# Attention heads in pairs with V stationary, and the output projection moved to a stage of its own

## The reference, cut to what matters

```python
oa = band_attend(qa, ka, va, ...)            # own chunk and 8 before: at most 640 keys a tile, bias table
score = sum_h wi[h] * relu(qi[h] . ki)       # indexer; keep the 256 best keys of each query
ob = softmax(qb . kb / 8 + t5_bias, on the kept keys) @ vb     # all keys up to the tile's end
y  = x + gate1 * rmsnorm(concat(oa, ob) @ w_out)
h  = rmsnorm(y) * (1 + scale2) + shift2
y  = y + gate2 * rmsnorm(swiglu(h, w_gate, w_up, w_down))
```

## Time and profile before

| | us |
|---|---|
| median of three runs (1856.07 to 1862.26) | 1858.51 |
| the profiled execution, its own time | 1858.22 |
| its span, first to last instruction | 1856.4 |
| PE busy, 9145 matmul rows | 1712.2 |
| DVE / ACT / POOL busy | 819.1 / 658.0 / 173.6 |
| mean granted PE clock, share of full speed | 0.961 |

### The profile page before, as it was taken

How to read it: one execution, slowest core, us unless ns; L and a number is a source line. 1 busy time by engine, 2 the same in 40 slices (tenths; PEclk the granted TensorE clock), 3 DMA queues, 4 the chain that set the end, 5 groups by cost and what they waited for, 6 DMA issues and landing times. The chain is left out here.

```text
span 1856.4 us, 23651 instructions
## 1 busy us (share of the span) xinstructions
PE 1712.2 (92%) x9145; PEld 1372.6 (74%) x9145; DVE 819.1 (44%) x1601; ACT 658.0 (35%) x1215; POOL 173.6 (9%) x299
## 2 busy tenths in 40 slices
PE   4998899999799988899999299999999999999997
PEld 0543899964578755566654299999999999787876
DVE  2111566668899865554432411111111111455454
ACT  2100445545899823333322511111111111343433
POOL 3001000033111011221100100000000000102020
PEclk9999899999799979999999699999999999999999
DMA  9445511140000030000000411111111111643442
GB/s 345 190 169 189 146 46 35 35 138 1 1 2 1 2 139 23 23 24 30 20 20 26 142 57 45 45 45 45 45 45 45 45 45 44 244 148 122 153 144 95
DMA packets 96850, 146.70 MB, mean 79 GB/s; under 512 B 12896, under 2 KB 71472, under 8 KB 94688
## 3 DMA queue, kind: packets, MB, share of 16 engines
q1 hardware_dynamic: 93408, 135.18, 21.9%
q0 software_dynamic: 3360, 10.43, 1.6%
HBM read 128.61 MB, written 18.95 MB: 79 GB/s over the span
## 5 line engine op out<-in xcount | busy, mean ns | idle before, releaser
L1408 PE MATMUL ps<-h_hi,w_hi 128*128 128x352 f32 x1056 | 341.6, 324 | 7.8 <-DVE w_lo L1448 7.8
L1408 PE MATMUL ps<-h_lo,w_hi 128*128 128x352 f32 x1056 | 339.3, 321 | 0.0
L1408 PE MATMUL ps<-h_hi,w_lo 128*128 128x352 f32 x1056 | 339.0, 321 | 0.0
L954 PE MATMUL ps<-arena 128*128 128x512 f32 (+5 forms) x464 | 183.3, 512 | 33.3 <-POOL arena L735 17.0
L1408 PEld LDWEIGHTS ps<-h_hi,w_hi 128*128 128x128 f32 x1056 | 198.9, 188 | 7.9 <-DVE w_lo L1448 7.9
L1408 PEld LDWEIGHTS ps<-h_lo,w_hi 128*128 128x128 f32 x1056 | 199.1, 189 | 0.0
L1408 PEld LDWEIGHTS ps<-h_hi,w_lo 128*128 128x128 f32 x1056 | 198.6, 188 | 0.0
L941 PE MATMUL ps<-arena 128*128 128x64 f32 (+2 forms) x1280 | 165.1, 266 | 8.5 <-DVE arena L1012 3.1
L941 PEld LDWEIGHTS ps<-arena 128*128 128x128 f32 (+2 forms) x1280 | 154.0, 185 | 13.1 <-ACT arena L1012 3.6
L1448 DVE TENSOR_TENSOR w_lo<-raw_weights,w_hi 128x1024 fp32r<-128x1024 f32 x44 | 53.6, 1221 | 233.7 <-ACT w_hi L1422 233.7
L954 PEld LDWEIGHTS ps<-arena 128*128 128x128 f32 (+1 forms) x464 | 79.1, 196 | 97.1 <-issue 66.1
(11 more groups left out here) (193 smaller groups left out, 2488.9 us busy)
## 6 DMA issues: line engine op xcount, KB each, us to landing
raw_weights<-in_w_down SPq DMA_DIRECT2D x66, 512.0 KB, 3.3
arena<-in_w_ada SPq DMA_DIRECT2D x24, 1024.0 KB, 9.8
raw_weights<-in_w_gate SPq DMA_DIRECT2D x22, 512.0 KB, 3.7
raw_weights<-in_w_up SPq DMA_DIRECT2D x22, 512.0 KB, 3.8
arena<-in_w_in SPq DMA_DIRECT2D x16, 512.0 KB, 3.7
arena<-in_x_prompt SPq DMA_DIRECT2D x4, 1024.0 KB, 18.6
arena<-in_w_out SPq DMA_DIRECT2D x2, 2048.0 KB, 10.3
arena<-in_x_prompt SPq DMA_DIRECT2D x8, 512.0 KB, 3.5
```

Source lines behind the costliest of these rows:

```text
L954: mm = nc.tensor.matmul(ps_cols(B, s_col(s) + lo, hi - lo, r), q, key_source(t, h, lo, hi), start=True, stop=True)
L1408: mm = nc.tensor.matmul(B(3 * i + c, CH), cut[i][a][:, P * k:P * k + P], h[:, NTOK * k + CH * c:NTOK * k + CH * (c + 1)], start=(k == 0 an ...
```

## The change

- **Pairs.** A step handles two heads (2c and 2c+1) of a tile: 36 pairs in place of 72 units. The queries are no longer copied into padded buffers; the product for each head uses only its own 64 partitions, head 2c on partitions 0 to 63 and head 2c+1 on 64 to 127, issued one after the other into different PSUM banks. Each head has one score area (banks 0-1, 2-3): pair s waits for both masks of pair s-1.
- **V stationary.** V (keys by 64 features) is loaded as weights and the transposed exponentials move, 128 columns (queries). The two heads' results go to partitions 0 to 63 and 64 to 127 of bank 7. They come out as [feature, token], so L1167, L979 and L1019 go; ACT copies bank 7 over the queries (`leave`).
- **Row sums.** PE transposes the 8 sums of a tile (item "R"), DVE takes the reciprocal, SP stores it to DRAM and loads it back spread over partitions, and POOL multiplies the tile in place.
- **Copies of transposed weights.** In the band part ACT copies those of the even head and DVE those of the odd one; in the sparse part ACT copies all. There are six SBUF slots in place of four.
- **Sample tile of the sparse part.** Keys 1024 to 1055 have their own ring item ("X") and their own small bias, minimum and merge.
- **`project_out`.** A new stage takes the place of the projection in the sparse part and of `ffn_input`: it loads w_out in 8 slabs of 512 KB through two buffers, cuts each (ACT high, DVE low), and per tile makes 48 fp32r products, the norms, y and the modulated, cut input of `gate_up`. One tile's head features are cut at a time.

The core of the diff:

```diff
+LAG, PV_LAG, RING_BANKS, SLOTS = 2, 2, 3, 6
+PAIRS = [(t, c) for t in range(NT) for c in range(HEADS // 2)]
...
-    pts = [KI, KI + 512, KIC, KIC + 512]
-    pbuf = [QI + 640 * i for i in range(4)] if band else [QI + NTOK * i for i in range(4)]
+    pts = [KI, KI + 512, KIC, KIC + 512] + ([QI + 3200, QI + 3712] if band else [HT, HT + 512])
+    pbuf = [QI + 640 * i for i in range(5)] if band else [QI + NTOK * i for i in range(4)] + [KA, KA + NTOK]
...
-        dve_reads = it[0] == "W" or (it[0] == "T" and it[2] > 0)
-        reader.append("v" if dve_reads else "a")
+    reader = ["a" if it[0] == "T" and (it[1] % 2 == 0 or not band) else "v" for it in items]
...
             for t in range(NT):
+                ring_read(sp, item_of[("R", t, 0, 0)])
+                sp.dma_start(d_r[t][:, 0:r], T(RT, r, HEADS)).then_inc(rinv_out, 16)
+                sp.wait_ge(rinv_out, 16 * t + 16)
+                for i in range(2):
+                    sp.dma_start(T3(BC, 4, P, HD, HD * i)[:, :, 0:r], src[:, 0:r].partition_broadcast(HD)).then_inc(rinv_in, 16)
...
-                    mm = nc.tensor.matmul(B(7, HD, r, c0=HD * h), T(pts[t_seq[q] % 4] + P * i, r, k),
-                                          value_source(t, h, b), start=(b == 0), stop=(b == blocks - 1))
+                    for i in range(2):
+                        mm = nc.tensor.matmul(B(7, r, HD, HD * i, c0=P * c), value_source(t, 2 * c + i, b),
+                                              T(pts[t_seq[qe + i] % SLOTS] + P * x, r, k), start=(b == 0), stop=(b == blocks - 1))
...
-                    pe.wait_ge(pad_ready, s + 3)
-                    q = T(pad_slot(pad, s), r)
-                    for lo, hi in pieces(0, width(t), 512):
-                        mm = nc.tensor.matmul(ps_cols(B, s_col(s) + lo, hi - lo, r), q, key_source(t, h, lo, hi),
+                    if s:
+                        pe.wait_ge(masked, 2 * s)
+                    for lo, hi in pieces(0, min(width(t), 1024), 512):
+                        for i in range(2):
+                            mm = nc.tensor.matmul(B(2 * i + lo // 512, hi - lo, r), T(q_at + NTOK * c + P * t, r, HD, HD * i),
+                                                  key_source(t, c, i, lo, hi), start=True, stop=True)
...
+def project_out(ctx, nc, ins, outs, sem, T, T3, B, view, ident, d_ada, d_y, h_hi, h_lo, raw, **_):
...
+            def load_w(c):
+                if c >= 2:
+                    sp.wait_ge(wo_lo, c - 1)
+                sp.dma_start(raw[c % 2], ins["w_out"][0][P * c:P * c + P, :]).then_inc(wo_in[c % 2], 16)
...
+        @block.tensor
...
+            for t in range(NT):
+                r = rows_of(t)
+                if t >= 2:
+                    pe.wait_ge(m_scaled, t - 1)
+                for c in range(KT):
+                    if t == 0:
+                        pe.wait_ge(wo_lo, c + 1)
+                    if c % 4 == 0:
+                        pe.wait_ge(o_lo, 2 * t + c // 4 + 1)
+                    for half in range(2):
+                        for n, (a, b) in enumerate(TERMS):
+                            mm = nc.tensor.matmul(B(2 * (t % 2) + half, 512, r), o_cut[a][:, P * c:P * c + r],
...
+                    if c % 4 == 3:
+                        mm.then_inc(half_mm, 1)
+                if t:
+                    turn(t - 1)
+            turn(SAMPLE)
+
+        @block.scalar
...
+            for t in range(NT):
+                r = rows_of(t)
+                if t + 1 < NT:
+                    first_cut(t + 1, 0)
+                    first_cut(t + 1, 1)
+                if t:
+                    act.wait_ge(turned, t)
...
+                act.wait_ge(half_mm, 2 * t + 2)
+                nc.scalar.activation(R(MB, D, r), mixed(t), ACT.Square, accum_out=T(R_SSM + t, 1, r)).then_inc(ssm_done, 1)
+                if t:
+                    h_first(t - 1)
+                act.wait_ge(y_done, t + 1)
+                nc.scalar.activation(R(MB, D, r), xb(t, r), ACT.Square, accum_out=T(R_SSY + t, 1, r)).then_inc(ssy_done, 1)
+                act.wait_ge(ry_done, t + 1)
+                act.wait_ge(ssy_done, t + 1)
+                nc.scalar.activation(R(MB, D, r), xb(t, r), ACT.Copy, scale=T(R_RY + t, 1, r)).then_inc(yn_done, 1)
...
-def ffn_input(ctx, nc, ins, outs, sem, T, T3, B, view, ident, d_y, hidden, h_hi, h_lo, raw, a_sample, **_):
```

More of the change, by code:

```diff
@@ L111, in pieces @@
     return out
[L114 to L133, removed]
 def build(nc, ins, outs):
@@ L891, in block_rows, with scores, normalised @@
         return min(P, width(t) - P * b)
[L893 to L907, removed]
+    def scores(u, n):
+        t = PAIRS[u // 2][0]
+        return B(2 * (u % 2), n, rows_of(t))
+    def normalised(eng, t):
+        eng.wait_ge(normed, t + 1)
     with nc.Block() as block:
@@ L991, in _ @@
+                if s >= NP + LAG and pending:
                     pv(pending.pop(0))
         def read_item(eng, name, q):
-            it = items[q]
-            bank = 4 + q % RING
+            kind, u, b0, nb = items[q]
+            bank = 4 + q % RING_BANKS
             eng.wait_ge(ring_mm, q + 1)
@@ L998, in read_item @@
             done = ring_act if name == "a" else ring_dve
-            if it[0] == "T":
-                _, u, b0, nb = it
-                t = units[u][0]
+            if kind == "T":
+                t = PAIRS[u // 2][0]
                 r = rows_of(t)
                 i = t_seq[q]
-                if i >= 4:
-                    eng.wait_ge(pv_mm, i - 3)
-                full = [b for b in range(nb) if block_rows(t, b0 + b) == P]
-                part = [b for b in range(nb) if block_rows(t, b0 + b) < P]
-                dst, src = T(pts[i % 4], 512), B(bank, 512)
-                assert not (full and part), "a ring item is full blocks or one partial block"
-                if full:
-                    copy(view(dst, [[P, len(full)], [1, r]]), view(src, [[P, len(full)], [1, r]])).then_inc(done, 1)
+                if i >= SLOTS:
+                    eng.wait_ge(pv_mm, i // 2 - SLOTS // 2 + 1)
+                dst, src = T(pts[i % SLOTS], 512), B(bank, 512)
+                if block_rows(t, b0) == P:
+                    copy(view(dst, [[P, nb], [1, r]]), view(src, [[P, nb], [1, r]])).then_inc(done, 1)
@@ L1385, in gate_up, with _ @@
         block = own.enter_context(nc.Block())
+        @block.gpsimd
+        def _(pool):
+            nc.gpsimd.memset(a_sample[:, :].bitcast(F32), 0.0).then_inc(zeroed, 1)
         @block.sync
         def _(sp):
+            for n in range(2):
+                load_down(sp, ins, raw, n).then_inc(wd_in[slot(n)], 16)
             with sp.Fori(1, FT) as f:
```

628 lines of the change are left out of this document (345 added, 283 removed).

## The result

The changed kernel takes 1827.45 us (median) against 1858.27 for the kernel before in the same comparison: ratio 0.9833, 95% interval 0.9809 to 0.9856. That is 31 us faster where 90 were forecast, and outside the range (1742 to 1814). The profiled execution spans 1823.7 us against 1856.4, so 32.7 of the forecast 90 are to be found in the traces, and 57.3 are missing.

The account below looks back on a forecast made before the run. Band part bound by PE, DVE and ACT together, sparse part by PE alone, `ffn_input` by a DRAM round trip and a chain. Band +7, sparse -198, `project_out` +101 give -90: 1858.2 to 1768 us, range 1742 to 1814.

Parts of the forecast that it names:

- With 15 of its present 19.5 idle, 194: +7: Band part: DVE busy 179 us plus 15 idle gives 194, 7 longer than before.
- With five SBUF buffers ...: nothing: Band part: the odd head's mask also waits for a transpose of its own step, at no cost.
- DVE ... is the limit: Band part: DVE's bisection and masks set the pace, so relieving PE buys nothing.
- Nine reads of row sums: Band part: DVE's nine reads at about 0.29 us each add 2.6 us.
- 157, 9 and 10: Sparse part: 157 us for tiles and sample, 9 for bank 7 and lower-clock stretches, 10 at the end; stated result 177.
- 23.5: Sparse part: time in us for the sample, set by PE.
- Wrong altogether would be a handover that I hold to be covered: Sign that would refute the forecast: a wait costed at nothing, on the single score area or three-bank ring.
- The scores run in turn: Rival, sparse part: the two heads' score products do not overlap, 24 us more, 1792 in all; chance 20%.
- V stationary saves nothing: Rival, sparse part: V products stay at 0.42 us a block of both heads, 1786 in all; chance 4%.
- the chain of `project_out`: Rival: the chain beside PE's products sets the pace at 15 us a tile, 22 more, 1790; chance 13%.
- the lower clock: Rival, both attention parts: 64-wide products leave PE at 1.2 GHz, doubling its time, 1895 in all; chance 4%.
- nothing, at most 6.6: Start of `gate_up`: two w_down loads ahead of weights cost nothing, at most 6.6 us.

Follow-up runs that it names:

- experiment 5: ACT's counts in the band part moved to a later step, handover kept, against the changed kernel: band part 198.9 us.
- experiments 2 and 6: Sixth probability buffer in the band part, added to the changed kernel (band part 215.5 us), then to the kernel with moved counts (199.2 us).
- experiment 7: Changed kernel with moved counts and six buffers, plus ACT copying first groups of transposed weights and DVE the second ones: band part 183.7 us.
- experiment 9: X items put behind the first transposes and `raw_weights` 64 columns longer, against the changed kernel: sparse part 187.5 us, `gate_up` 514.6.
- Experiments 9 to 11: Changed kernel with `gate_up` operands moved stepwise to the addresses of the kernel before, besides other edits: `gate_up` 514.6, 515.7 and 515.5 us.

## Why the prediction was wrong

- **Band part, the step that failed: "With 15 of its present 19.5 idle, 194: +7".** The work was right in sum (DVE 179.0 of 179 forecast); idle became 42.5. I took the idle time of the kernel before over to a plan with another order. The pair plan runs two thirds of a bisection round in each step, and in every second round ACT's counts stand at the end of the very step in which DVE makes their threshold. I gave this no term at all. Moving the counts alone gives back 22.6 of the 27.9 missing (experiment 5); what remains is 199 against 194, idle of 20 where I said 15.
- **"With five SBUF buffers ...: nothing"** was right in substance: 6 us while ACT is late, nothing once it isn't (experiments 2 and 6).
- **"DVE ... is the limit"** holds once the handover is mended: 14.5 us off DVE are 15.5 off the part (experiment 7).
- **Nine reads of row sums "at about 0.29"** are mis-sized, 7.9 us for 2.6. That DVE's sum was right all the same is luck: the masks took 45.6 for 47.8, the reciprocals of the kernel before (1.7), which go, weren't counted, and the copies grew by 13.5 where 15 stood. A group of the changed kernel's band part, and the reciprocal of the kernel before:

```profile
L1027 DVE RECIPROCAL small<-ps 8x128 f32<-8x128 f32 (+1 forms) x9 | 7.9, 876 | 2.5 <-PE ps L999 2.5
```

```profile
L1162 DVE RECIPROCAL small<-small 128x8 f32<-128x8 f32 (+1 forms) x9 | 1.7, 192 | 0.0
```

- **Sparse part.** By its own terms (157, 9 and 10) the forecast's sum is 176, not 177. **Tiles 0 to 7** are right to 1 us, by DVE to tile 5 and by PE after it; for PE's tiles this is partly luck, since a block of V products takes 0.22 where 0.24 stood and the changes about 0.7 a pair where 0.33 stood. **The sample was mis-sized** at "23.5": I priced PE's rows and not the two banks that its X items hold while DVE works through its masks one after the other, nor the lower clock of its later pairs. Sample and end took 52.95 where 34.5 stood (with the sample's 1 us), and 42.85 in experiment 9, whose tiles 0 to 7 took 2.2 longer, so that its sparse part is only 7.9 shorter. "Wrong altogether would be a handover that I hold to be covered: the single score area, or the ring of three banks": it was the ring, here. **The end** took 17.75, not 10: the trip through DRAM and back is 6 as forecast (the last transposes of row sums at 884.93, the next stage at 891.07), but what is left of the last pair's step and the two pairs of lag drain at a granted clock of 0.50 in 11.6 where 4 stood. No run here separates the clock from the chain of transposes, copies and products in it.
- **`project_out`** is right: tile 0's products end 28.5 us after the start (27 forecast), tiles then follow every 11.8 as forecast, and PE never waits for the chain between tiles. Its waits in this stage are the slabs at the start, one turn at the very end and `gate_up`'s first weights:

```profile
PE ps L1295 <- DVE wo_lo_w L1362: 16.4, 6, 10.2
PE ps L1281 <- ACT out_work L1337: 8.1, 1, 8.1
```

- **Rivals.** "The scores run in turn" and "V stationary saves nothing" fall by the timeline of tile 7; the chain of `project_out` by its waits. For the scores the Trainium skill (TensorEngine Tiling, Theoretical Speedup) offers up to 2x for a contraction of 64, and the trace agrees nearly: 3.54 us in turn, twice the 1.77 of the earlier trace rows, against 1.92, or 1.84x. The Trainium skill's other rule there (TensorEngine Tiling, Key Properties) is that a change of tiling mode drains the engine. The trace agrees that a change costs something: about 0.15 each at tile 7, an estimate from its rows, near the 0.17 of my price, and some 0.7 for a pair's five, where that price made 1.0 of six; that this is a drain, no run here shows. As to the lower clock, that column-group products "raised the clock" in the earlier trace rows was read off their lengths alone, for the profile's granted clock is 1.00 in both stretches; but such products ran all through tile 7 at 1.00. The lower clock came, 0.75 and 0.84 on average, but it isn't what made the band part long: with the counts moved 22.6 us went at a granted clock still of 0.79.
- **`gate_up`: "nothing, at most 6.6"** was priced at its start, and there it is nothing (PE begins 2.36 after ACT's first cut of weights in both kernels). But the same 3168 products take longer throughout. Before and after:

```profile
1067.65:1573.30 505.65, 505.65 (x3167) 505.65 (x3168) 81.33 (x109) 69.80 (x112) 0.00 (x0) 1.00 0.15 46
```

```profile
1028.40:1543.80 515.40, 515.40 (x3168) 515.40 (x3168) 81.40 (x109) 69.78 (x112) 0.00 (x0) 1.00 0.16 46
```

  One product every 0.1596 us became one every 0.1627, at a granted clock of 1.00 in both, in every kernel of this study with the new stages (514.6 to 515.7). Experiments 9 to 11 put the operands back to their old addresses without effect. What costs these 9.8 us stays open; the raw slots and `silu_gate` still lie elsewhere, which wasn't tried. (`down` gives 3 of them back.)

## What to carry to other kernels

When two steps of a plan are merged into one, look for every chain that crosses engines with a period counted in steps, and follow one round of it through the new order: the busiest engine's time can be right to a microsecond and the stage still a seventh longer than forecast. An engine that waits at the end of its step makes everything queued behind that wait late, so work whose input comes late in a step goes into the next one. And an item that holds a bank of a small ring until a slow reader has come round belongs behind those whose reader is quick.

## What the hardware showed that I had not expected

- A reciprocal of 8 x 128 took 0.95 us on DVE and one of 128 x 8, as many elements, 0.19 on average with the sample's: the time seems to follow the length of a row (the sample's 8 x 32 took 0.35). The first reads PSUM and the other SBUF; no run here has both shapes from one of them.
- Products of 64-row halves do run side by side: 1.92 us for twice the rows that took 1.77.
- Going from scores to transposes to products with V and back costs PE about 0.15 us a time (an estimate from the rows of tile 7), for the transposes too, which are the same as before.
- The same instructions of the band part took 183.7 or 187.7 us, with granted clocks of 0.84 and 0.79, in two kernels that differ only in later stages.
- A uniform 2% on `gate_up`'s products at full granted clock that none of the moved addresses explains.
